# Three queue edits in a decoder step: first weight block all on SP's queue, window cache in 1 KB rows, one GpSimd wait removed

## The reference, cut to what matters

```python
u = x @ w_in     # q | compressed KV | selected KV | window KV | 24 gates | recurrent branch | merge gates
...
past_c = pool_c[page_table].reshape(Bd, PAST_LEN, 2, N_KV_HEADS, HEAD_DIM)   # 2048 rows a sequence
kc, vc = compress(past_c + new row)            # 127 compressed keys and values a sequence
rows_w = jnp.concatenate([win_buf, kv_w], axis=1)                            # 512 cached rows + 1
m_w = (diff >= 0) & (diff <= WINDOW) & (w_pos[None, :] >= 0)                 # all 513 rows pass
s_w = einsum(q_rot, kv_w keys) * scale;  o_w = masked_softmax(s_w, m_w) @ kv_w values
```

## Time and profile before

| | us |
|---|---|
| median of 3 runs | 2119.32 |
| lowest, highest | 2119.08, 2125.03 |
| profiled execution: its own time | 2119.32 |
| profiled execution: its span | 2117.3 |
| PE busy in it | 2043.3 (97%) |
| DVE, POOL, ACT busy | 1033.1, 653.7, 586.9 |

### The profile page before, as it was taken

The page is one execution under the profiler, slowest core; times in us unless marked ns, Lnnn a source line. Parts: engine busy times, 40 slices in busy tenths (PEclk is TensorE's granted clock), DMA queues, the critical chain, the costliest instruction groups (busy, mean ns, idle before and its releaser), DMA issues.

```text
span 2117.3 us, 28320 instructions
## 1 busy us (share of the span) xinstructions
PE 2043.3 (97%) x9812; PEld 1276.6 (60%) x9812; DVE 1033.1 (49%) x2070; ACT 586.9 (28%) x1294; POOL 653.7 (31%) x810
## 2 busy tenths in 40 slices
PE   8998999999999999999999999999999999999997
PEld 6454665667788878888885556444444444444442
DVE  3226888653676683454444558532323233232334
ACT  1125777525255551111112220011111111111114
POOL 0004565521000000000000000366666666566562
PEclk9999999899999999999999999999999999999998
DMA  7312000267211111123204124899999999999966
GB/s 229 121 32 99 2 2 2 103 256 302 61 40 27 34 40 42 31 58 108 64 20 146 60 100 184 305 378 364 368 341 349 346 371 340 344 355 365 357 179 242
DMA packets 151391, 379.38 MB, mean 179 GB/s; under 512 B 34131, under 2 KB 96295, under 8 KB 127595
## 3 DMA queue, kind: packets, MB, share of 16 engines
q1 hardware_dynamic: 118275, 292.11, 37.1%
q0 software_dynamic: 30576, 84.40, 13.7%
q10 hardware_dynamic: 2432, 1.41, 0.2%
HBM read 343.58 MB, written 58.00 MB: 190 GB/s over the span
## 4 chain that ended last, share of the span: by engine, by line
PE 75%; SPq 7%; DMA 6%; DVE 5%; ACT 3%; issue 3%; POOL 0%; DVEq 0%; ACTq 0%; POOLq 0%
PE PS L1331 20%; PE PS L1561 14%; PE PS L1572 6%; PE PS L1470 5%; PE PS L982 5%; DMA arena<-in_w_exp_down 5%; SPq L760 4%; PE PS L1454 3%; PE PS L1018 2%; PE PS L871 2%; PE PS L1055 2%; PE PS L1146 2%; SPq L768 2%; PE PS L876 2%; PE PS L1632 2%
## 5 line engine op out<-in xcount | busy, mean ns | idle before, releaser
L1331 PE MATMUL PS<-arena 128*128 128x258 f32 x2352 | 514.7, 381 | 2.9 <-DVE arena L2451 2.7
L1331 PEld LDWEIGHTS PS<-arena 128*128 128x128 f32 x2352 | 445.6, 190 | 70.2 <-issue 3.1
L1561 PE MATMUL PS<-arena 128*128 128x512 f32 x1040 | 459.7, 595 | 14.6 <-DMA arena<-in_w_exp_down 8.6
L1658 ACT ACTIVATE arena<-PS 128x512 f32<-128x512 f32 (+10 forms) x461 | 199.3, 446 | 650.2 <-PE PS L1331 238.2
L1561 PEld LDWEIGHTS PS<-arena 128*128 128x128 f32 x1040 | 192.7, 190 | 257.6 <-issue 240.2
L2843 POOL DMA_INDIRECT arena<-x_rows,tokall x276 | 276.6, 1002 | 166.5 <-DVE tokall L2682 96.2
L1572 PE MATMUL PS<-arena 128*128 128x512 f32 x520 | 233.9, 592 | 0.5 <-ACT arena L1658 0.5
L2827 POOL MEMSET arena<- 128x2 f32 x1 | 0.1, 99 | 743.9 <-PE PS L1470 743.9
L2701 DVE TENSOR_TENSOR arena<-PS,arena 128x256 f32<-128x256 f32 x65 | 27.6, 424 | 331.1 <-ACT arena L2010 180.4
L1572 PEld LDWEIGHTS PS<-arena 128*128 128x128 f32 x520 | 96.4, 191 | 109.2 <-issue 108.6
L2695 DVE STREAM_TRANSPOSE arena<-arena 128x1024 f32<-128x1024 f32 x67 | 135.7, 2025 | 43.2 <-DMA arena<-x_rows,tokall 42.8
(11 more groups left out here) (343 smaller groups left out, 2304.9 us busy)
## 6 DMA issues: line engine op xcount, KB each, us to landing
arena<-in_w_exp_down SPq DMA_DIRECT2D x65, 1024.0 KB
arena<-in_w_exp_gate SPq DMA_DIRECT2D x55, 1024.0 KB
arena<-in_w_exp_up SPq DMA_DIRECT2D x55, 1024.0 KB
arena<-in_w_in SPq DMA_DIRECT2D x33, 512.0 KB, 5.2
expert_rows<-arena SPq DMA_DIRECT2D x16, 512.0 KB
arena<-in_w_exp_gate SPq DMA_DIRECT2D x10, 768.0 KB
arena<-in_w_exp_up SPq DMA_DIRECT2D x10, 768.0 KB
arena<-in_x_prompt SPq DMA_DIRECT2D x9, 512.0 KB
```

The source lines that it names most:

```text
L1331: ins = mm(PS[:, bank, 0:QT], lhs[:, l0 + k, :], right[:, r0 + k, c0:c0 + QT], start=first and k == 0, stop=k == kh - 1, skip_group_check= ...
L1561: ins = mm(PS[:, 2 + s, :].rearrange("p (h n) -> p h n", h=2), xgT[:, s, k, :], chunk(w, k), start=k == 0, stop=k == KT - 1)
L1658: return fn(out, in_, ACT.Copy)
```

## The change

Three edits, in three engines' programs.

1. The two later parts of `wta` move from the head of ACT's queue to SP's queue, behind the first part and ahead of SP's x quarters. PE's wait for all three stays.
2. The window cache is laid out with row t*128 + p in partition p (before: row 4p + t). A partition's 4 KB are then four pieces of 1 KB from four places, where they were one piece.
3. POOL no longer waits for the window transfers before it gathers page set 5.

```diff
@@ block.sync
             sp.dma_start(xin[:, 0, :], a["x_prompt"][0:P, :]).then_inc(s_x[0], 16)
-            sp.dma_start(wta[:, 0:4, 0:KV], w_in_rows[:, 0:4, QW:QW + KV]).then_inc(s_wta, 16)
+            for h in range(2):
+                sp.dma_start(wta[:, 4 * h:4 * h + 4, 0:KV], w_in_rows[:, 4 * h:4 * h + 4, QW:QW + KV]).then_inc(s_wta, 16)
+            sp.dma_start(wta[:, :, KV:KV + 24], w_in_rows[:, :, QW + 3 * KV:TOKW]).then_inc(s_wta, 16)
             for t in range(1, 4):
                 x_tile(sp, t, (0, 1))
@@ block.sync, at the start of decode
             for b in range(BD):
-                sp.dma_start(wKV[:, b, :, :], a["win"][b].rearrange("(p t) c -> p t c", p=P)).then_inc(sem("win_in"), 16)
+                sp.dma_start(wKV[:, b, :, :], a["win"][b].rearrange("(t p) c -> p t c", p=P)).then_inc(sem("win_in"), 16)
@@ block.scalar
-            act.dma_start(wta[:, 4:8, 0:KV], w_in_rows[:, 4:8, QW:QW + KV]).then_inc(s_wta, 16)
-            act.dma_start(wta[:, :, KV:KV + 24], w_in_rows[:, :, QW + 3 * KV:TOKW]).then_inc(s_wta, 16)
             for t in range(1, 4):
                 x_tile(act, t, (2, 3))
@@ block.gpsimd
             for b in range(2, BD):
                 if b >= 4:
                     pool.wait_ge(sem("dh_done"), b - 3)
-                if b == 5:
-                    pool.wait_ge(sem("win_in"), 16 * BD)
                 pages_in_four(b)
```

## The result

The changed kernel takes 2134.5 us (median of 6 runs, 2132.15 to 2137.91), the kernel before 2120.95 us in the same rounds (2116.75 to 2125.03). The ratio is 1.0062, 95% interval 1.0047 to 1.0078: slower by 13.1 us, between 10.0 and 16.5. Forecast were 2128.4 and a range up to 2134.0. So the direction came out, and so did the mechanism in decode; the size did not, nor the mechanism at the start.

A forecast was written before the change was run, and what follows sets the result against it. TensorE was taken to bound the kernel, three quarters of the chain, its start set by the last weight part. Start +2.4 and decode +6.7 sum to 9.1 us; 2119.3 + 9.1 = 2128.4 us, range 2114.9 to 2134.

The forecast's parts named there:

- window turn: Decode: PE's first window turn at 446.3 instead of 441.76, after an 11.3 us wait for the window transfers.
- half clock behind it: Decode, after PE's long stop: work at half clock for some 4.4 us, costing 2.2 us.
- Both together move about 420 GB/s ... so pages some 340, window 85: Decode: page and window queues alternate piece by piece, 4 KB against 1 KB, so pages get four fifths of the bandwidth.
- Alone, the queue gets 244 GB/s for window data: Decode: rate of the window queue in 1 KB pieces when no pages flow.
- Left 0.6 MB, alone at 244: 2.2 us: Decode: window data remaining when the pages end at 444.1, so the window lands at 446.3.
- the upper bound: Decode: at a mixed rate of 380 GB/s instead of 425, pages end 3.7 us later, making decode +10.4 us.
- Two queues of 1 KB pieces together move 379 GB/s, one alone 244: Start: queue rates used to time the weight parts on SP's queue, giving +2.4 us on `project_cmp`'s start.
- rival A: Start costs nothing because only bytes count, while the window is late: 2126.0 us; chance 12%.
- the start's own bound (4.8): Start: +4.8 us if the gate columns, alone, go no faster than 318 pieces in a us.
- B: Decode: window keeps its share, page set 2 lands at 425 and decode changes by 0: 2121.7 us; chance 14%.
- C: Decode: pages gain, window complete by 435.0, PE runs through; -4.4 us with the start's cost, 2114.9; chance 8%.
- D: Decode: set 6 comes after the window, which lands at 442.3; PE 0.6 us late, clock 2.2: 2124.5; chance 8%.

The follow-up runs named there:

- start_only: Kernel before with only the first edit, all three weight parts on SP's queue: ratio 1.0017.
- start_x_behind: Kernel before with all three weight parts on SP's queue, and ACT holding its six x quarters until the weights are in: ratio 1.0021.
- both_held: Kernel before with all weight parts on SP, ACT's x quarters after the first x tile, last 5 of 8 window transfers held until page set 2 landed: ratio 0.9979.
- rows_nowait: Kernel before with window rows in 1 KB pieces and POOL's wait before page set 5 removed, start unchanged: ratio 1.0051.
- wait_set6: Kernel before with window rows in 1 KB pieces and POOL's wait for the window moved from page set 5 to set 6: ratio 1.0013.
- window_late: Kernel before, 4 KB window pieces, with SP holding the last 5 of 8 window transfers until page set 2 has landed: ratio 0.9986.
- Part 3: Run alone: kernel before with only POOL's wait before page set 5 removed, window still in 4 KB pieces: ratio 0.9995.
- rows_only: Kernel before with only the window rows in 1 KB pieces, POOL's wait before page set 5 kept: ratio 0.9998.
- window_hold4: Kernel before, 4 KB window pieces, with SP holding the last 4 of 8 window transfers until page set 2 has landed: ratio 0.9990.

## Why the prediction was wrong in size, right in kind for decode, and wrong on the start

**The chain of decode, step by step.** Times from the start of decode, 407.63 in the working, and 413.75 in the changed kernel.

| step | forecast | measured |
|---|---|---|
| set 2 landed | +12.4 | +13.6 |
| gap before `cmp_out(0)` | 0 | 0.72 |
| PE ready for the window | +27.4 | +28.9 |
| PE's wait for it | 11.3 | 12.7 |
| window turn | +38.7 | +41.6 |
| half clock behind it | 2.2 | 2.5 |

Every event came, in its order. The step that failed is "Both together move about 420 GB/s ... so pages some 340, window 85": together they move 401 from 424 to 432 us (2.52 + 0.69 MB in 8 us), pages 315 and the window 86, and over the whole stretch from 419 to 453 pages 306 and the window 90. The lower number was there to be read: the earlier trace rows has 2.31 + 2.45 MB in 12 us, 397 GB/s, of which four fifths are 317. I took the 417 of a window in which almost only pages flowed. Whether the smaller pieces slow the mix as well can't be seen from 401 against 397: over 2 us the rate varied between 338 and 426 in the stretch of the earlier trace rows, and between 366 and 414 from 420 to 452 us of the changed kernel.

Sets 2 to 6 then take 34 us and not 30.9; they began 0.4 us sooner than forecast, at +5.2 and not +5.6, so they end 2.7 us late, and the window turn is 2.9 late. Two more terms were wrong and hardly show. "Alone, the queue gets 244 GB/s for window data": from 417 to 418 the window alone moved 377. And "Left 0.6 MB, alone at 244: 2.2 us": nearly nothing was left when the pages ended, yet the window landed 2 us later; that this equals the forecast's 2.2 is luck, and what the last 0.04 MB waited for is open.

The working named this error as the upper bound (mixed rate 380, +10.4 us for decode), and the measured decode is +8.7 against 92.6, inside it.

**The start.** The forecast was +2.4; measured are +3.3 (changed kernel) and +2.7 (start_only) at `project_cmp`, against 10.2, then +2.5 and +3.4 at the second projection, against 48.5, and 3.6 us in start_only's ratio. So the size is about right, but by luck, since the reason was wrong: the step "Two queues of 1 KB pieces together move 379 GB/s, one alone 244". Both numbers are of x quarters, and the sum used them for weights. Weights alone on one queue move 375. They became slow since ACT's x quarters, no longer behind weights, shared the engines with them. With them held back `project_cmp` starts at 8.85 (start_x_behind) and 8.67 (both_held). By the rule of the Trainium skill, DMA: Bandwidth & Descriptors, section Issuing engines are not separate DMA queues, the choice of queue gives no bandwidth. For the weights start_x_behind agrees with it. For the x quarters no run does: 379 GB/s on two queues, 213 to 244 on one. And rival A, which made the cost 0 of this rule, is out, because the edit also changed what runs beside what. What makes an x quarter slow is open: it fills 32 partitions and a weight part 128, and no run changed that alone.

**The sum.** 2.4 + 6.7 = 9.1 forecast. By the stages it is about 3 (between 2.5 and 3.4) + 8.7 = 11.7; by the ratios of start_only and rows_nowait 3.6 + 10.8 = 14.4; measured 13.1 (10.0 to 16.5). Two things put it past the range's end. The range took the upper bound of decode (10.4) with the middle of the start (2.4) and not with the start's own bound (4.8). And it stood on 2119.3, the median of three executions, which was low: the median of before was 2120.95 in the rounds with the changed kernel, and 2121.9 to 2123.7 in the later ones. Upon 2120.95 the same width of 14.7 us ends at 2135.6.

**The rivals.** A (the start costs nothing) is out by start_only, B (equal shares of the bytes) by 694 to 689. C and D didn't happen in the changed kernel, but other orders of the queues give what they describe. D's mechanism, set 6 behind the window, is wait_set6: forecast at 0.6 + 2.2 us of loss, measured at 2.4 in decode (1.6 of it in `cmp_hidden(2)`) and 2.8 by the ratio. C's gain without the loss is window_late.

**Part 3** alone costs nothing, as said, and decides over some 10 us when the rows are in 1 KB pieces (rows_nowait against rows_only).

## What to carry to other kernels

Where two queues both had work throughout decode, they moved equal numbers of pieces (694 and 689, 586 and 586), so the size of a piece set each transfer's share of the bandwidth: small pieces go to the queue that may wait. Count the pieces before relying on it, for at the start the counts could be unequal (236 and 98). Ask of every wait that seems to cost time what it keeps out of a queue, for a transfer that is needed later can push back one that is needed sooner. And before forecasting a change of half a per cent from one profile, allow for stages that vary by 2 to 4 us from one execution to the next.

## What the runs showed of the hardware

- Pieces of 1 KB alone in one queue moved at 375 GB/s (weights, 128 partitions a transfer), 377 (window rows, 128 partitions, 417 to 418 us of the changed kernel) or 213 GB/s (x quarters, 32 partitions), with the engines' share full in all three.
- Two full queues had 694 and 689 packets (3.6 against 1.0 KB a packet), 586 and 586 (3.7 against 1.9 KB).
- SP's 8 issues of 512 pieces lasted 19.08 us, where 8 of 128 took 4.96 us.
- ACT stood still for 8.0 us in rows_only, 10.8 us in window_hold4 and 3.5 us in wait_set6 (before 433.62), and no instruction or transfer of the kernel ended it. What did is open.
- A gap of PE of 1.10 us was followed by a granted clock of 0.50 in wait_set6, one of 2.00 us by 1.00 in rows_only.
- Attention, the same code in all 14 kernels, took 360.0 to 363.9 us.
